# Moving the normalised activations to other byte offsets, with a shifted copy for the low-part products

## Chip, cores and metric

One Trainium2 chip, one NeuronCore. The metric is the device time of one execution in microseconds; less is better. The kernel before takes 793.53 us (median of 3 runs, 793.42 to 794.03). The granted TensorE clock of the profiled execution is 1.000 throughout, the 2.4 GHz level.

## What is computed

Two transformer blocks on 256 tokens of width 1024, everything in float32:

```python
# first_block: 16 meta tokens in front
h = h + concat([pool, forgetting_attention, stick_breaking_attention]) @ w_out
h = h + (silu(a @ w_gate) * (a @ w_up)) @ w_down      # a = rmsnorm(h)
# second_block
x = x + 0.5 * rmsnorm(swiglu(rmsnorm(x), w_ffn1_in, w_ffn1_out))
x = x + rmsnorm(mixer(rmsnorm(x)))                    # convolution and mLSTM
x = x + 0.5 * rmsnorm(swiglu(rmsnorm(x), w_ffn2_in, w_ffn2_out))
```

So there are three FFNs with hidden width 2816, an attention block and a mixer. Activations and weights enter each product split into two parts of float32r, hi and lo, and three of the four partial products are summed: hi by hi, hi by lo, lo by hi.

## The kernel before

**Weights.** All large weights come as a stream of 129 units of 128 x 2048 float32 (1 MB), which SyncE loads into three slots `raw`. For every unit ScalarE writes `whi` (a rounding copy, L695) and VectorE writes `wlo = raw - whi` (L1023), three slots each. `hi_ready`, `lo_ready` and `unit_used` count units made and used.

**An FFN** (`ffn(f)`, f = 0, 1, 2) has 11 groups of 256 hidden columns; a group is a gate unit, an up unit and a down unit of weights. TensorE (`ffn` in the tensor block) takes them in an order written out by hand: the first gate unit (`first_paired_unit`), up(0), then group(1) written out flat, then groups 2 to 10 as a hardware loop (`pe.Fori`), each group being gate(g), up(g), down(g - 1), and a last down unit. In gate and up

- `hi_products` are 16 matmuls with 512 moving columns: the moving operand is `xn[norm][:, kt, :, :]`, the hi and lo block of one k-tile next to each other, the stationary operand a 128 x 128 slice of `whi`;
- `lo_products` are 16 matmuls with 256 moving columns: the moving operand is the hi block `xn_hi[norm][:, kt, :]`, the stationary operand a slice of `wlo`.

In down (`rows_tile`) the roles are the other way round: 24 matmuls whose moving operand is 512 columns of `whi` or `wlo` and whose stationary operand is a slice of `hhi` or `hlo`.

**The mixer** has 12 weight units. Ten of them go through `columns_tile` or `first_columns_unit` (48 matmuls each, 256 moving columns of `xn_hi[2]` or `xn_lo[2]`, stationary slices of `whi` or `wlo`); the two units of kind "v" go through `tokens_tile` (48 matmuls each, moving 256 columns of the weights, stationary slices of `xn_hi[2]` and `xn_lo[2]`).

**Where things lie.** `raw`, `whi`, `wlo` (three each, 8192 bytes a partition), `xa` (17408) and `ya` (16384), `hhi` and `hlo` (2048 each) are allocated one after the other, and every size is a multiple of 512 bytes. So all of them start at the same residue of the byte address modulo 512. A weight slice starts a multiple of 512 bytes into its buffer: it is at "the weights' residue", called residue 0 here. Other operands are given by how many bytes past it they start, modulo 512. The normalised activations of norm k lie in `xa`, from element `XN_AT[k][0]` on, and k-tiles follow each other every 2048 bytes, hi block first, lo block 1024 bytes behind it. `XN_AT` is 80 elements for all four norms, which is residue 320. The `hhi`, `hlo` and `ya` slices that serve as stationary operands of down and out are at residue 0.

**ScalarE at the head of an FFN** (`ffn` in the scalar block): the whi copy of unit0 + 2 (`split_ahead(unit0)`), `gate_lo` (L875) that takes the first gate product out of PSUM, in the second and third FFN two `root_of_x` (L705 to L735), a table load (L896), the whi copy of unit0 + 3, `up_lo` (L883), the whi copy of unit0 + 4, the silu of group 0 (L879). VectorE's wlo of unit0 + 3 waits for that whi copy, and behind it on VectorE stands `up(0)` (L1278), for which TensorE's up(1) waits (`up_out`).

```python
XN_AT = ((80, SEQ),) * 4
        for at, far in XN_AT:
            line = xa_line[:, at:at + KT * 2 * SEQ if far == SEQ else at + 2 * far]
```

Of the kernel before, what the change touches and what calls it, by code (L numbers as in the profile page):

```python
# [31 lines left out]
F32 = mybir.dt.float32  # L32
F32R = mybir.dt.float32r
ALU = mybir.AluOpType
ACT = mybir.ActivationFunctionType
# [4 lines left out]
KT = D // P  # L40
META = 16
SEQ = 256
# [3 lines left out]
GROUPS = FF // 256  # L46
UNIT = 2048
SLOTS = 3
XN_AT = ((80, SEQ),) * 4
XN_HI = (0, 0, 0, 0)  # L50
EPS = 1e-6
NEG = -1e30
# [218 lines left out]
def build_blocks(nc, x_in, meta_in, wstream, ident_in, vecs_in, small_in, const_in, rows_in, out):  # L271
    with ExitStack() as ctx:  # L272
# [3 lines left out]
        def sem(name):  # L276
            return ctx.enter_context(nc.semaphore(name))


        ps = ctx.enter_context(nc.psum_tensor("ps", [P, 8, 512], F32))  # L280
        raw = [sb(f"raw{s}", [P, UNIT]) for s in range(SLOTS)]
        whi = [sb(f"whi{s}", [P, UNIT], F32R) for s in range(SLOTS)]
        wlo = [sb(f"wlo{s}", [P, UNIT], F32R) for s in range(SLOTS)]
        xa = sb("xa", [P, KT, 2 * TOK], F32R)
        ya = sb("ya", [P, KT, 2 * SEQ], F32R)
# [144 lines left out]
        xn_hi = [xn[k][:, :, n, :] for k, n in enumerate(XN_HI)]  # L430
        xn_lo = [xn[k][:, :, 1 - n, :] for k, n in enumerate(XN_HI)]

        xa_hi, xa_lo = xa[:, :, 0:TOK], xa[:, :, TOK:2 * TOK]
        ps_line = ps[:].rearrange("p b c -> p (b c)")

# [10 lines left out]
        unit_used = sem("unit_used")  # L446
# [30 lines left out]
        xa_hi_ready = sem("xa_hi_ready")  # L477
# [78 lines left out]
        up_lo_out = sem("up_lo_product_out")  # L556
        up_out = sem("up_out_of_psum")
        silu_done = sem("silu_done")
        h_done = sem("h_done")
        hhi_done = sem("h_hi_done")  # L560
        hlo_done = sem("h_lo_done")
# [120 lines left out]
        def _(act):  # L682
# [14 lines left out]
            def split_ahead(n):  # L697

                if n + 2 < UNITS:
                    split(n + 2, (n + 2) % SLOTS, (n + 2) // SLOTS)  # L700
# [167 lines left out]
            def ffn(f):  # L868
                base, unit0 = f * GROUPS, U_FFN[f]

                def gate_lo(g, unit):
                    act.wait_ge(unit_used, unit + 1)
                    if not isinstance(g, int) or base + g:
                        act.wait_ge(h_done, g + base)
                    nc.scalar.activation(silu, products(4)[1], ACT.Copy).then_inc(gate_lo_out, 1)  # L875

                def gate(g):
                    act.wait_ge(gate_scaled, g + (base + 1))
                    nc.scalar.activation(silu, silu, ACT.Silu).then_inc(silu_done, 1)  # L879

                def up_lo(unit):
                    act.wait_ge(unit_used, unit + 1)
                    nc.scalar.activation(up_sum, products(6)[1], ACT.Copy).then_inc(up_lo_out, 1)  # L883

                def hidden_hi(g, down_before, last=False):
                    act.wait_ge(h_done, g + (base + 1))
                    if down_before is not None and not last:
                        act.wait_ge(unit_used, down_before + 1)
                    nc.scalar.activation(ya[:, 0:2, 0:SEQ] if last else hhi[:], hact, ACT.Copy).then_inc(hhi_done, 1)  # L889

                split_ahead(unit0)
                gate_lo(0, unit0)
                if f:
                    for tt in range(TT):
                        root_of_x((0, 1, 3)[f], tt)
                nc.scalar.preload_act_table_set("silu_and_others")  # L896
                split_ahead(unit0 + 1)
                up_lo(unit0 + 1)
                split_ahead(unit0 + 2)
                gate(0)  # L900
                hidden_hi(0, None)

                def group(g, last=False):

                    for j in range(3):

                        n = g * 3 + (unit0 - 1 + j)
                        c = unit0 + 1 + j
                        if last and j == 2:
                            hidden_hi(g, n, True)  # L910
                        if isinstance(g, int):
                            if n != unit0 + 2:
                                split_ahead(n)
                        else:
                            split(n + 2, c % SLOTS, g + c // SLOTS)
                        if j == 0:
                            gate_lo(g, n)
                        if j == 1:
                            gate(g)
                            up_lo(n)  # L920
                        if j == 2 and not last:
                            hidden_hi(g, n)

                group(1)
                with act.Fori(2, GROUPS - 1) as g:
                    group(g)
                group(GROUPS - 1, True)
                nc.scalar.preload_act_table_set("natural_log_exp_and_others")  # L928
                split_ahead(unit0 + N_FFN - 1)
# [15 lines left out]
            for kind, i in SECOND:  # L945
                if kind in ("munit", "mout"):
                    split_ahead((U_MIX if kind == "munit" else U_MIXOUT) + i)
                if kind == "munit":
                    what = MIX_KIND[i]
                    if what == "v":  # L950
                        act.wait_ge(root_ready, R_BEFORE[2] + 2 * TT)
                        act.wait_ge(unit_used, U_MIX + i + 1)
                        for tt in range(TT):
                            ins = nc.scalar.activation(mv[:, tt, (i - 2) * SEQ:(i - 1) * SEQ], two(UNIT_BANK[i])[:, tt, :], ACT.Copy,
                                                       scale=stat[:, S_RSTD[2] + tt:S_RSTD[2] + tt + 1])
# [32 lines left out]
                if kind == "ml_weigh":  # L988
                    act.wait_ge(decay_row, 1)
                    act.wait_ge(ml_scored, i + 1)  # L990
                    for tt in range(TT):
                        for dr in range(2):
                            _, d, n = DIRECTION[tt, dr]
                            ins = nc.scalar.activation(dm[:, tt, d:d + n], ps[:, 4 + tt, d:d + n], ACT.Exp,
                                                       bias=max_neg[:, tt, dr, i:i + 1])
# [480 lines left out]
        def _(pe):  # L1476
            def mm(o, lhsT, rhs, start, stop):
                return nc.tensor.matmul(o, lhsT, rhs, start=start, stop=stop, skip_group_check=True)  # L1478
# [310 lines left out]
            def ffn(f):  # L1789
                base, unit0 = f * GROUPS, U_FFN[f]  # L1790

                norm = (0, 1, 3)[f]

                def hi_products(bank, slot, start, spread=False):

                    for kt in range(KT):
                        if spread and kt == KT // 2:
                            spread_rstd(norm, 2)
                        for a in range(2):
                            w = slice(kt * 256 + a * P, kt * 256 + (a + 1) * P)  # L1800
                            ins = mm(two(bank + a), whi[slot][:, w], xn[norm][:, kt, :, :], start and kt == 0, not start and kt == KT - 1)
                    return ins

                def lo_products(bank, slot, start):

                    for kt in range(KT):
                        for a in range(2):
                            w = slice(kt * 256 + a * P, kt * 256 + (a + 1) * P)
                            ins = mm(ps[:, bank + a, 0:SEQ], wlo[slot][:, w], xn_hi[norm][:, kt, :], start and kt == 0, not start and kt == KT - 1)
                    return ins  # L1810

                def gate(g, unit, slot, first):
                    pe.wait_ge(gate_out, g + base)
                    pe.wait_ge(hi_ready, unit)
                    hi_products(4, slot, True, first)
                    pe.wait_ge(lo_ready, unit + 1)
                    lo_products(4, slot, False).then_inc(unit_used, 1)

                def up(g, unit, slot):
                    if not isinstance(g, int) or g:  # L1820
                        pe.wait_ge(up_out, g + base)
                    pe.wait_ge(lo_ready, unit + 1)
                    lo_products(6, slot, True)
                    hi_products(6, slot, False).then_inc(unit_used, 1)

                def down(g, unit, slot, first, last):

                    pe.wait_ge(lo_ready, unit + 1)
                    pe.wait_ge(hlo_done, g + (base + 1))
                    for a in range(2):  # L1830
                        ins = rows_tile(slot, a, hhi[:, a, :], hlo[:, a, :], first and a == 0, last and a == 1)
                    ins.then_inc(unit_used, 1)

                pe.wait_ge(lo_ready, unit0 + 1)
                first_paired_unit(4, unit0 % SLOTS, norm).then_inc(unit_used, 1)
                up(0, unit0 + 1, (unit0 + 1) % SLOTS)

                def group(g, first):
                    n = g * 3 + (unit0 - 1)
                    gate(g, n, (unit0 + 2) % SLOTS, first)  # L1840
                    up(g, n + 1, unit0 % SLOTS)
                    down(g - 1, n + 2, (unit0 + 1) % SLOTS, first, False)

                group(1, True)
                with pe.Fori(2, GROUPS) as g:
                    group(g, False)
                n = unit0 + N_FFN - 1
                pe.wait_ge(lo_ready, n + 1)
                pe.wait_ge(hlo_done, base + GROUPS)
                rows_last_unit(n % SLOTS, [(ya[:, a, 0:SEQ], ya[:, a, SEQ:2 * SEQ]) for a in range(2)], (1, 2, 4)[f])  # L1850
# [175 lines left out]
```

## Time and profile before

| what | value |
|---|---|
| median of 3 runs | 793.53 us |
| profiled execution, its own time | 793.85 us |
| its span, first to last instruction | 792.0 us |
| TensorE busy | 781.6 us |
| VectorE / ScalarE busy | 533.2 us / 429.3 us |
| DMA | 141.16 MB, 178 GB/s over the span |

A matmul in the trace has a start and a modelled end, and the matmuls overlap, so what a product costs TensorE is read from starts: the time from one start to a later one, divided by the number of products between (called the pace here). A row of the timeline merges equal neighbours; its first number is the start of the first, its last the count.

### The profile page before, as it was taken

What the parts mean: (1) busy time and instruction counts of PE and PEld (TensorE: products, weight loads), DVE (VectorE), ACT (ScalarE), POOL (GpSimd) and SP (SyncE); (2) the same over time, 40 slices, a digit from 0 to 9 for tenths busy, and PEclk for the clock granted to TensorE, in tenths of its full rate; (3) what the DMA queues carried; (4) which work ended last, traced back from release to release, by engine and by line L of the source; (5) the groups of instructions that cost most, each with busy time, mean ns of one, the idle gap of its engine ahead of it and who ended that gap; (6) DMA issues with size and microseconds to landing.
All of it is one profiled execution on the core that took longest, in us unless ns stands there. A gap on an engine that the chain in (4) does not pass through costs nothing.

```text
span 792.0 us, 12209 instructions
## 1 busy us (share of the span) xinstructions
PE 781.6 (99%) x4710; PEld 687.9 (87%) x4710; DVE 533.2 (67%) x628; ACT 429.3 (54%) x565; POOL 28.3 (4%) x35
## 2 busy tenths in 40 slices
PE   9999999999999999999999999999999999999997
PEld 8989988888888888888888887999988888888885
DVE  7866657766666667866666566766977766666665
ACT  6556657544544448744544447565557654454444
POOL 0000000000000000000000000002520000000000
PEclk9999999999999999999999999999999999999999
DMA  9633433645555553665545554452444664555521
GB/s 335 235 110 112 143 115 128 245 166 205 191 183 209 175 196 110 238 224 199 198 176 209 183 188 159 142 204 108 161 165 162 221 223 166 205 192 183 208 106 54
DMA packets 20797, 141.16 MB, mean 178 GB/s; under 512 B 2448, under 2 KB 2704, under 8 KB 4384
## 3 DMA queue, kind: packets, MB, share of 16 engines
q1 hardware_dynamic: 20192, 138.65, 48.8%
q0 software_dynamic: 576, 2.10, 0.8%
q8 instruction: 21, 0.34, 0.2%
q14 instruction: 8, 0.07, 0.0%
HBM read 139.69 MB, written 1.05 MB: 178 GB/s over the span
## 4 chain that ended last, share of the span: by engine, by line
PE 94%; ACT 2%; DVE 2%; issue 1%; DMA 1%; SPq 0%; DVEq 0%; ACTq 0%
PE ps L1478 93%; ACT whi L695 1%; PE ps L1484 1%; DMA raw<-wstream 1%; DVE x L1227 0%; ACT squared L710 0%; DVE xa L1034 0%; PE ps L1707 0%; DVE wlo L1023 0%; PE ps L1677 0%; PE ps L1926 0%; DVE xg L1222 0%; DVEq L272 0%; ACT L928 0%; PE ps L1709 0%
## 5 line engine op out<-in xcount | busy, mean ns | idle before, releaser
L1478 PE MATMUL ps<-xa,whi 128*128 128x512 f32 (+2 forms) x1744 | 377.4, 347 | 0.0
L1023 DVE TENSOR_TENSOR wlo<-raw,whi 128x2048 fp32r<-128x2048 f32 x128 | 293.6, 2295 | 82.2 <-ACT whi L695 82.2
L1478 PEld LDWEIGHTS ps<-xa,whi 128*128 128x128 f32 x1744 | 299.6, 188 | 41.4 <-issue 2.1
L695 ACT ACTIVATE whi<-raw 128x2048 fp32r<-128x2048 f32 x128 | 244.2, 1909 | 6.9 <-PE ps L1478 6.8
L1478 PE MATMUL ps<-xa,wlo 128*128 128x256 f32 (+1 forms) x1376 | 219.8, 278 | 0.0
L1478 PEld LDWEIGHTS ps<-xa,wlo 128*128 128x128 f32 x1376 | 187.9, 188 | 2.8
L1478 PE MATMUL ps<-wlo,hhi 128*128 128x512 f32 x240 | 93.5, 390 | 0.0
L1478 PE MATMUL ps<-whi,hlo 128*128 128x512 f32 x240 | 93.5, 390 | 0.0
L1478 PE MATMUL ps<-whi,hhi 128*128 128x512 f32 x240 | 93.5, 390 | 0.0
L889 ACT ACTIVATE hhi<-arena 128x512 fp32r<-128x512 f32 x30 | 19.0, 633 | 88.4 <-PE ps L1478 81.9
L875 ACT ACTIVATE arena<-ps 128x512 f32<-128x512 f32 x33 | 19.7, 597 | 85.5 <-PE ps L1478 85.4
L883 ACT ACTIVATE arena<-ps 128x512 f32<-128x512 f32 x33 | 19.7, 597 | 71.4 <-PE ps L1478 71.4
L1478 PE MATMUL ps<-whi,ya 128*128 128x512 f32 x176 | 56.5, 395 | 0.0
L1478 PEld LDWEIGHTS ps<-whi,hhi 128*128 128x128 f32 x240 | 45.1, 188 | 9.6
L1478 PEld LDWEIGHTS ps<-wlo,hhi 128*128 128x128 f32 x240 | 45.1, 188 | 9.5
L1478 PEld LDWEIGHTS ps<-whi,hlo 128*128 128x128 f32 x240 | 45.1, 188 | 9.5
L1269 DVE TENSOR_TENSOR arena<-ps,arena 128x512 f32<-128x512 f32 x33 | 22.8, 691 | 39.6 <-ACT arena L875 39.6
L1278 DVE TENSOR_TENSOR arena<-ps,arena 128x512 f32<-128x512 f32 x33 | 22.8, 691 | 36.6 <-ACT arena L883 36.6
L1290 DVE TENSOR_TENSOR hlo<-arena,hhi 128x512 fp32r<-128x512 f32 x30 | 20.8, 692 | 37.8 <-ACT hhi L889 37.7
L1478 PEld LDWEIGHTS ps<-whi,ya 128*128 128x128 f32 x176 | 33.1, 188 | 6.8
L1478 PE MATMUL ps<-wlo,ya 128*128 128x512 f32 x88 | 34.5, 393 | 0.0
L1478 PE MATMUL ps<-arena 64*128 64x144 f32 (+11 forms) x190 | 24.3, 340 | 1.8 <-DVE arena L1067 1.3
(221 smaller groups left out, 531.6 us busy)
## 6 DMA issues: line engine op xcount, KB each, us to landing
raw<-wstream SPq DMA_DIRECT2D x128, 1024.0 KB, 4.8
gain_row<-rows_in POOLq DMA_DIRECT2D x4, 512.0 KB, 3.9
x<-x_in SPq DMA_DIRECT2D x2, 512.0 KB, 4.0
raw<-wstream SPq DMA_DIRECT2D x2, 512.0 KB, 5.8
out<-x SPq DMA_DIRECT2D x4, 256.0 KB, 2.1
xg<-const_in SPq DMA_DIRECT2D x1, 912.0 KB, 11.8
small<-small_in SPq DMA_DIRECT2D x1, 152.0 KB, 6.1
arena<-meta_in SPq DMA_DIRECT2D x1, 64.0 KB, 4.5
```

Of the source, the lines that this page charges most:

```text
L695: nc.scalar.activation(whi[slot][:], raw[slot][:], ACT.Copy).then_inc(hi_ready, 1)
L875: nc.scalar.activation(silu, products(4)[1], ACT.Copy).then_inc(gate_lo_out, 1)
L883: nc.scalar.activation(up_sum, products(6)[1], ACT.Copy).then_inc(up_lo_out, 1)
L889: nc.scalar.activation(ya[:, 0:2, 0:SEQ] if last else hhi[:], hact, ACT.Copy).then_inc(hhi_done, 1)
L1023: nc.vector.tensor_tensor(wlo[slot][:], raw[slot][:], whi[slot][:].bitcast(F32), ALU.subtract).then_inc(lo_ready, 1)
L1269: nc.vector.tensor_tensor(silu, products(4)[0], silu, ALU.add).then_inc(gate_out, 1)
L1278: nc.vector.tensor_tensor(up_sum, products(6)[0], up_sum, ALU.add).then_inc(up_out, 1)
L1290: nc.vector.tensor_tensor(lo, hact, hi.bitcast(F32), ALU.subtract).then_inc(hlo_done, 1)
L1478: return nc.tensor.matmul(o, lhsT, rhs, start=start, stop=stop, skip_group_check=True)
L1484: ins = nc.tensor.transpose(turn_place(k, kt)[:, tt * P:(tt + 1) * P], x[:, tt, kt * P:(kt + 1) * P], ident[:])
```

## The change

The normalised activations of the three FFNs (norms 0, 1 and 3) move to residue 0, those of the mixer (norm 2) to residue 192. At the head of each FFN ScalarE copies the eight hi blocks into `ya`, 16 elements in, so that the copy lies at residue 64; it is one ACTIVATE of 128 x 2048, and it waits for the hi blocks and for the last unit before the FFN to be used. From group 1 on the lo products take their moving operand from this copy; the first unit and up(0) take it from `xn_hi` as before. TensorE waits for the copy once in each FFN, ahead of the lo products of group 1.

```diff
-XN_AT = ((80, SEQ),) * 4
+XN_AT = ((0, SEQ), (0, SEQ), (48, SEQ), (0, SEQ))
+FAR = 16
...
+        x_far = ya[:, :, FAR:FAR + SEQ]
...
                 split_ahead(unit0)
+                act.wait_ge(xa_hi_ready, KT * ((0, 1, 3)[f] + 2))
+                act.wait_ge(unit_used, unit0)
+                nc.scalar.activation(x_far, xn_hi[(0, 1, 3)[f]].bitcast(F32), ACT.Copy).then_inc(far_ready, 1)
                 gate_lo(0, unit0)
...
-                def lo_products(bank, slot, start):
+                def lo_products(bank, slot, start, of):
...
-                            ins = mm(ps[:, bank + a, 0:SEQ], wlo[slot][:, w], xn_hi[norm][:, kt, :], start and kt == 0, not start and kt == KT - 1)
+                            ins = mm(ps[:, bank + a, 0:SEQ], wlo[slot][:, w], of[:, kt, :], start and kt == 0, not start and kt == KT - 1)
...
                     pe.wait_ge(lo_ready, unit + 1)
-                    lo_products(4, slot, False).then_inc(unit_used, 1)
+                    if first:
+                        pe.wait_ge(far_ready, f + 1)
+                    lo_products(4, slot, False, x_far).then_inc(unit_used, 1)
...
-                    lo_products(6, slot, True)
+                    lo_products(6, slot, True, xn_hi[norm] if isinstance(g, int) and g == 0 else x_far)
```

No instruction moves against another on any engine apart from the three added ones. ScalarE at the head of the second FFN, before (whi copy of unit0 + 2, gate_lo, the two roots, table load, whi copy of unit0 + 3, up_lo):

```order
179 L695 ACTIVATE whi<-raw 128x2048 [waits unit_used,unit_landed1]
180 L875 ACTIVATE arena<-ps 128x512 [waits h_done,unit_used]
181 L705 ACTIVATE squared,stat<-x 128x1024 [waits x_written]
182 L733 ACTIVATE stat<-stat,eps 128x1 [waits act_step]
183 L735 ACTIVATE stat<-stat 128x1 [waits act_step]
184 L705 ACTIVATE squared,stat<-x 128x1024 [waits x_written]
185 L733 ACTIVATE stat<-stat,eps 128x1 [waits act_step]
186 L735 ACTIVATE stat<-stat 128x1 [waits act_step]
187 L896 ACT_TABLE_LOAD
188 L695 ACTIVATE whi<-raw 128x2048 [waits unit_used,unit_landed2]
189 L883 ACTIVATE arena<-ps 128x512 [waits unit_used]
```

and in the change (line numbers behind the edits are 3 to 8 higher):

```order
180 L698 ACTIVATE whi<-raw 128x2048 [waits unit_used,unit_landed1]
181 L897 ACTIVATE ya<-xa 128x8x256 [waits unit_used,xa_hi_ready]
182 L878 ACTIVATE arena<-ps 128x512 [waits h_done,unit_used]
183 L708 ACTIVATE squared,stat<-x 128x1024 [waits x_written]
184 L736 ACTIVATE stat<-stat,eps 128x1 [waits act_step]
185 L738 ACTIVATE stat<-stat 128x1 [waits act_step]
186 L708 ACTIVATE squared,stat<-x 128x1024 [waits x_written]
187 L736 ACTIVATE stat<-stat,eps 128x1 [waits act_step]
188 L738 ACTIVATE stat<-stat 128x1 [waits act_step]
189 L902 ACT_TABLE_LOAD
190 L698 ACTIVATE whi<-raw 128x2048 [waits unit_used,unit_landed2]
191 L886 ACTIVATE arena<-ps 128x512 [waits unit_used]
```

The copy stands between the first whi copy and gate_lo, and all that follows stands behind it. TensorE in the same FFN, from up(0) to the first products of down(0), before:

```order
762 L1478 MATMUL ps<-xa,wlo 128x256 x15
763 L1478 MATMUL ps<-xa,whi 128x512 x16
764 L1478 MATMUL ps<-xa,whi 128x512 [waits unit_hi_ready,gate_out_of_psum]
765 L1478 MATMUL ps<-xa,whi 128x512 x7
766 L1478 MATMUL ps<-diag,exact 128x128 [waits diag_ready] x2
767 L1478 MATMUL ps<-xa,whi 128x512 x8
768 L1478 MATMUL ps<-xa,wlo 128x256 [waits unit_lo_ready]
769 L1478 MATMUL ps<-xa,wlo 128x256 x15
770 L1478 MATMUL ps<-xa,wlo 128x256 [waits unit_lo_ready,up_out_of_psum]
771 L1478 MATMUL ps<-xa,wlo 128x256 x15
```

and in the change:

```order
767 L1484 MATMUL ps<-xa,whi 128x512 x8
768 L1484 MATMUL ps<-ya,wlo 128x256 [waits far_copy_of_hi_activations_ready,unit_lo_ready]
769 L1484 MATMUL ps<-ya,wlo 128x256 x15
770 L1484 MATMUL ps<-ya,wlo 128x256 [waits unit_lo_ready,up_out_of_psum]
771 L1484 MATMUL ps<-ya,wlo 128x256 x15
```

The same products in the same order: the moving operand of the lo products is `ya` now, and the first of them has one more semaphore to wait for.

## Rows read from the trace of the kernel before

**Rows 1.** The page: busy time of each engine, and the chain that ended last

```profile
PE 781.6 (99%) x4710; PEld 687.9 (87%) x4710; DVE 533.2 (67%) x628; ACT 429.3 (54%) x565; POOL 28.3 (4%) x35
...
PE 94%; ACT 2%; DVE 2%; issue 1%; DMA 1%; SPq 0%; DVEq 0%; ACTq 0%
```

**Rows 2.** Timeline of TensorE, one loop iteration: start, us, line, names, form, count

```profile
154.77 3.84 PE L1478 MATMUL ps<-xa,whi 128*128 128x512 f32 x16
158.45 3.79 PE L1478 MATMUL ps<-xa,wlo 128*128 128x256 f32 x32
162.08 3.82 PE L1478 MATMUL ps<-xa,whi 128*128 128x512 f32 x16
165.74 0.39 PE L1478 MATMUL ps<-whi,hhi 128*128 128x512 f32 x1
...
171.19 3.84 PE L1478 MATMUL ps<-xa,whi 128*128 128x512 f32 x16
```

**Rows 3.** Groups of TensorE by form: names, count, busy us, mean ns

```profile
L1478 PE MATMUL ps<-xa,whi 128*128 128x512 f32 x1008 | 241.7, 392 | 0.0
L1478 PE MATMUL ps<-xa,wlo 128*128 128x256 f32 x1264 | 189.3, 277 | 0.0
```

**Rows 4.** Timeline of TensorE, up(0) and group 1 of the second FFN (flat code)

```profile
317.42 5.67 PE L1478 MATMUL ps<-xa,whi 128*128 128x512 f32 x24
...
325.21 3.93 PE L1478 MATMUL ps<-xa,wlo 128*128 128x256 f32 x32
328.98 0.39 PE L1478 MATMUL ps<-xa,whi 128*128 128x512 f32 x1
```

**Rows 5.** Timeline of TensorE, first and last-but-one row of a mixer columns unit

```profile
536.55 0.40 PE L1478 MATMUL ps<-xa,whi 128*128 128x256 f32 x2
...
542.08 0.28 PE L1478 MATMUL ps<-xa,wlo 128*128 128x256 f32 x1
```

**Rows 6.** Timeline of TensorE, second and last row of both v units

```profile
510.72 0.28 PE L1478 MATMUL ps<-wlo,xa 128*128 128x256 f32 x1
...
516.14 0.28 PE L1478 MATMUL ps<-whi,xa 128*128 128x256 f32 x1
...
517.04 0.28 PE L1478 MATMUL ps<-wlo,xa 128*128 128x256 f32 x1
...
522.25 0.28 PE L1478 MATMUL ps<-whi,xa 128*128 128x256 f32 x1
```

**Rows 7.** Timeline of TensorE: an attention q tile, then the first unit of FFN 1

```profile
57.67 0.28 PE L1478 MATMUL ps<-xa,wlo 128*128 128x256 f32 x1
...
60.15 0.28 PE L1478 MATMUL ps<-xa,wlo 128*128 128x256 f32 x1
...
127.58 0.28 PE L1478 MATMUL ps<-xa,wlo 128*128 128x256 f32 x1
...
130.19 1.98 PE L1478 MATMUL ps<-xa,whi 128*128 128x256 f32 x16
```

**Rows 8.** Timeline of ScalarE, then of VectorE, head of the second FFN; idle in brackets

```profile
313.72 1.90 ACT L695 ACTIVATE whi<-raw 128x2048 fp32r<-128x2048 f32 x1
...
316.73 1.06 ACT L705 ACTIVATE squared<-x 128x1024 f32<-128x1024 f32 x1 [0.40 <-DVE x L1247]
...
321.37 1.91 ACT L695 ACTIVATE whi<-raw 128x2048 fp32r<-128x2048 f32 x1
323.19 0.58 ACT L883 ACTIVATE arena<-ps 128x512 f32<-128x512 f32 x1
...
323.38 2.29 DVE L1023 TENSOR_TENSOR wlo<-raw,whi 128x2048 fp32r<-128x2048 f32 x1 [1.82 <-ACT whi L695]
325.59 0.68 DVE L1278 TENSOR_TENSOR arena<-ps,arena 128x512 f32<-128x512 f32 x1
```

**Rows 9.** Timeline of ScalarE, heads of the first and of the third FFN

```profile
137.93 0.60 ACT L883 ACTIVATE arena<-ps 128x512 f32<-128x512 f32 x1 [1.89 <-PE ps L1478]
...
610.73 0.60 ACT L875 ACTIVATE arena<-ps 128x512 f32<-128x512 f32 x1 [1.72 <-PE ps L1478]
```

More of the change, by code:

```diff
@@ L558, in build_blocks @@
         silu_done = sem("silu_done")
+        far_ready = sem("far_copy_of_hi_activations_ready")
         h_done = sem("h_done")
```

## Prediction

> **What bounds the kernel.** I read the page's busy shares first and then its chain of waits [rows 1]: TensorE is busy for 781.6 of 792.0 us and makes up 94% of the chain that ended last. Nothing waits longer than TensorE works, so a change counts by what it does to the pace of TensorE's products, or by a wait that it puts in front of them. The modelled lengths (392 ns, 277 ns) overlap and say nothing of a pace [rows 3], so the next view is the timeline, by starts.
>
> One loop iteration of an FFN [rows 2]: the gate's 16 hi products take 158.45 - 154.77 = 3.68 us, 230.0 ns each; the 32 lo products of gate and up 3.63 us, 113.4 ns each; the up's 16 hi products 3.66 us, 228.8 ns each; the 24 products of down 5.45 us, 227.1 ns each. Hi products and down products have the same 512 moving columns. The first have their moving operand at residue 320 against the slice that is loaded for the next product, the second at residue 0. Twice a lo product is 226.8 ns, so down runs at what seems to be the floor, and the hi products about 2.3 ns above it.
>
> With 256 moving columns the picture is less simple. At residue 320 they run at 113.4 ns in the loop [rows 2], and the same products with the same slots in the flat group 1 at 3.77 us / 32 = 117.8 ns [rows 4]. Flat code can be fast too: the first unit of FFN 1 (residue 320, flat) takes 2.61 us / 23 = 113.5 ns a product [rows 7]. The mixer's columns unit (residue 320) takes 5.53 us / 47 = 117.7 ns [rows 5]; all of the columns units but the first look like it. The v units have moving weights against stationary activations, residue 192: the first takes 5.42 us / 46 = 117.8 ns, the second 5.21 us / 46 = 113.3 ns [rows 6]. So there are two steady paces, a short one (113.3) and a long one (117.8), a whole unit stays in one of them, and something besides the residue picks which. That is the weak spot of this forecast.
>
> **The change part by part.**
>
> *FFN hi products from residue 320 to 0.* There are 1008 [rows 3]. Their mean is (230.0 + 228.8) / 2 = 229.4 ns, down's is 227.1 [rows 2]. I take down's value, because it has the same shape, the same weight buffers and the residue to which they go: 1008 x 2.3 ns = -2.3 us. Ends: 0, if the residue isn't the reason, and 1008 x 2.7 = -2.7 us, if they reach 226.7. The copy at residue 64 plays no part in it. All of it is on the path.
>
> *Loop lo products from 320 to 64.* 27 iterations x 32 = 864 products. 320 and 64 differ by 256 bytes. The trace has no run of 256-column products at 64 alone; in the attention tiles, where the residue runs through 0, 64, 128 and on, nothing sets 64 apart from 320 [rows 7]. I take no change, 0; ends: 0 and, if they fall to the long pace, 864 x 4.4 = +3.8 us. The 96 lo products of the flat group 1 stay at 117.8 [rows 4]; end: the short pace, -0.4 us.
>
> *First unit and up(0) from 320 to 0.* 64 products with 256 columns in each FFN, flat, now at residue 0, which is only bounded by the attention q tile, whose products go through residues 0, 64, 128 and on: 2.48 us / 21 = 118.1 ns [rows 7]. The tile is the nearest row; I take it, with 0.5 ns for what it mixes in: 118.6. Of the 192 products some 40 (FFN 1's first unit behind its waits) are at 113.5 now, the other 152 at 117.8: 40 x 5.1 + 152 x 0.8 = +0.3 us. Ends: all short, -0.7 us; all at 120 (the long pace and half as much again), +0.6 us.
>
> *Mixer from 320 to 192.* Ten columns units with 480 products. The first is at the short pace behind a wait, nine (432 products) at the long one [rows 5]. The only rows at residue 192 are the two v units, one long, one short [rows 6]; so I take half: 216 x 4.4 ns = -1.0 us. Ends: 0 and -1.9 us. The two v units themselves go from 192 to 320, which is what the columns units have now: the short one becomes long, 48 x 4.5 = +0.2 us; ends 0 and +0.2.
>
> *The copy.* Three ACTIVATEs of 128 x 2048. The whi copy has that shape: 1.91 us long, the next instruction starts 323.19 - 321.37 = 1.82 us behind it [rows 8]. What is behind it on ScalarE moves by up to 1.82 us. In the first FFN ScalarE has 1.89 us of idle time ahead of up_lo, in the third 1.72 us ahead of gate_lo [rows 9]: hidden, and with that cover gone the next instructions come about 0.1 us late, which no one waits for. In the second FFN the copy starts at 313.72 + 1.82 = 315.54, gate_lo at 317.36 and the first square of x 0.49 us later (gate_lo's pitch), 317.85 instead of 316.73; the 0.40 us of idle there [rows 8] is used up, and 1.1 us of delay is left. It carries over to the whi copy of unit0 + 3 (322.5), the wlo behind it on VectorE (324.5 to 326.8) and up(0), L1278, which ends at 325.59 + 0.68 + 1.1 = 327.4 instead of 326.3. TensorE's up(1) wants it 16 lo products into the run that starts at 325.21 [rows 4], at 325.21 + 16 x 0.1178 = 327.1. So TensorE waits about 0.35 us once: +0.35. Ends: 0 and +0.8 (delay of 1.5 us, if nothing of the idle time helps). The products behind it are late by the same wait, so I count no second one. The copy itself is ready some 8 us ahead of the wait for it, and raw slots, DMAs and the GpSimd queue see nothing.
>
> Sum: -2.3 + 0 + 0.3 - 1.0 + 0.2 + 0.35 = -2.45 us. From the profiled execution's own 793.85 us that is 791.4; it stands 0.3 us above the median of the runs, so for the median **791.1 us**. A measurement of this kernel can tell about 0.2%, 1.6 us, from no change.
>
> **Rivals.**
>
> *The long pace takes the loop.* In the loop the lo products run at the short pace at 320, in flat code mostly at the long one [rows 2, 4]; what picks it isn't seen. If they go into the long pace behind hi products at residue 0, or 64 isn't like 320, each of 864 costs 4.4 ns: +3.8 us. If the mixer finds no better pace either (+1.0), 791.1 + 3.8 + 1.0 = 795.9 us, slower than before. It decides from about 560 of the 864 products on, where 2.45 us are eaten. For it: the same products show both paces. Against it: all 27 iterations look like the one shown, and 64 is 320 less 256. Chance 0.12.
>
> *The mixer gains nothing, the rest holds.* Columns at 192 stay at 117.8 like the first v unit [rows 6], and the first units are at the costly end: 791.1 + 1.0 + 0.3 = 792.4 us. Chance 0.16.
>
> *Addresses don't matter.* Then the 2.3 ns of the hi products come from their place in the program (the first ones behind the loop's branch, the slots), and the change leaves only its copy: 793.53 + 0.35 = 793.9 us. Against it: the up's hi products don't stand behind a branch and are at 228.8 all the same [rows 2]. Chance 0.10. The Trainium skill says so in effect: "TensorE: Matmul & The Clock Gate", "Step-by-step: what each phase is for", has two independent SBUF read ports, and loading the next tile's weights takes no read bandwidth from the running matmul; "SBUF — State Buffer", "Who interferes with whom", has it that TensorE never waits on anyone. By that rule no residue would change a pace. The trace doesn't show that the ports are the cause of the two paces, but it shows the same product at 113.4 and at 117.8 ns [rows 2, 4], which the rule leaves unexplained.
>
> *All of the mixer and the flat group go short:* 791.1 - 1.0 - 0.5 = 789.6 us. Chance 0.07.
>
> **How the numbers follow.** The forecast has 0.55. Its own range is 790.0 to 792.3. The range for 8 in 10 goes down to 789.4, which takes in most of the good case, and up to 794.4, which takes in the mixer rival and the no-effect rival; the long-pace rival is left out. Faster by over 0.2% (under 791.9 us): forecast and good case, 0.55 + 0.07, less what of the forecast's own range lies above, plus a little of the mixer rival: 0.60. Within 0.2%: the mixer rival, the no-effect rival and the edges, 0.28. Slower: 0.12.
>
> **What would show it.** Hi products of the loop at 226.7 to 227.1 ns in gate and up, iterations shorter by about 32 x 2.3 = 0.07 us (16.42 us from gate to gate before, 16.35 after). Lo products in the loop still 113.4 ns; at 117.8 the long-pace rival is right. Mixer columns units of 48 products at 5.44 us (short) or 5.65 us (long), the v units at the long pace. In the second FFN one TensorE wait of some 0.35 us for L1278's successor in the middle of group 1's lo products, none in the other two. The forecast is wrong if hi products stay at 229, or if TensorE waits for ScalarE or VectorE anywhere by over 1 us.

## The result, and the profile after

The change takes 795.82 us (median of 12 runs, 795.5 to 796.34) against 793.83 us of the kernel before on the same chip (12 runs, 793.42 to 794.37): a ratio of 1.0025, 95% interval 1.0018 to 1.0033. It is slower by 0.25%. The profiled execution took 796.34 us, with a span of 794.4 us.

The page of the change, busy time of each engine and the chain that ended last:

```profile
PE 783.3 (99%) x4710; PEld 691.1 (87%) x4710; DVE 533.0 (67%) x628; ACT 434.9 (55%) x568; POOL 28.3 (4%) x35
...
PE 88%; DVE 4%; ACT 3%; issue 2%; POOL 1%; DMA 1%; SPq 0%; DVEq 0%; ACTq 0%; POOLq 0%
```

Beside [rows 1] TensorE has the same 4710 products and 1.7 us more work, ScalarE 5.6 us more (its three copies). The chain now takes detours over VectorE, ScalarE and GpSimd, but TensorE is still busy nearly all the time, so the pace decides again. The same loop iteration as in [rows 2], by the timeline of TensorE (start, us, line, names, form, count):

```profile
155.10 3.79 PE L1484 MATMUL ps<-xa,whi 128*128 128x512 f32 x16
158.72 3.93 PE L1484 MATMUL ps<-ya,wlo 128*128 128x256 f32 x32
162.50 3.82 PE L1484 MATMUL ps<-xa,whi 128*128 128x512 f32 x16
166.15 0.39 PE L1484 MATMUL ps<-whi,hhi 128*128 128x512 f32 x1
...
171.59 0.61 PE L1484 MATMUL ps<-xa,whi 128*128 128x512 f32 x2
```

| part of the iteration | before, from [rows 2] | after | difference |
|---|---|---|---|
| gate hi, 16 | 3.68 us | 3.62 us, 226.3 ns each | -0.06 |
| lo, 32 | 3.63 us, 113.4 ns each | 3.78 us, 118.1 ns each | +0.15 |
| up hi, 16 | 3.66 us | 3.65 us, 228.1 ns each | -0.01 |
| down, 24 | 5.45 us | 5.44 us | -0.01 |
| gate to gate | 16.42 us | 16.49 us | +0.07 |

Times 27 iterations the row differences are about +1.9 us, which is all of the loss. Taken over every start in the 27 iterations the lo products went from 113.3 to 117.9 ns (864 of them: +3.9 us), the hi products from 229.4 to 227.55 ns on the mean (864: -1.6 us) and down's from 227.2 to 226.7 ns (648: -0.3 us): +2.0 us. A row's start is rounded to 0.01 us, so a pace read from one row's length is good to about 0.6 ns for 16 products and 0.3 ns for 32; where tenths of a nanosecond matter, means over all 27 iterations are given.

The second FFN, TensorE from the hi products ahead of group 1's lo products on (the counterpart of [rows 4]):

```profile
324.35 2.09 PE L1484 MATMUL ps<-xa,whi 128*128 128x512 f32 x8
326.28 4.18 PE L1484 MATMUL ps<-ya,wlo 128*128 128x256 f32 x32
330.30 2.00 PE L1484 MATMUL ps<-xa,whi 128*128 128x512 f32 x8
```

ScalarE there, in the change (the counterpart of [rows 8]):

```profile
316.51 1.91 ACT L897 ACTIVATE ya<-xa 128x2048 fp32r<-128x2048 f32 x1
...
323.42 1.92 ACT L698 ACTIVATE whi<-raw 128x2048 fp32r<-128x2048 f32 x1
```

and VectorE:

```profile
325.43 2.29 DVE L1029 TENSOR_TENSOR wlo<-raw,whi 128x2048 fp32r<-128x2048 f32 x1 [2.47 <-ACT whi L698]
327.64 0.68 DVE L1284 TENSOR_TENSOR arena<-ps,arena 128x512 f32<-128x512 f32 x1
```

The copy is the row at 316.51. Behind it the whi copy of unit0 + 3 comes at 323.42 instead of 321.37, 2.05 us later, while TensorE's lo products come 1.07 us later (326.28 instead of 325.21): ScalarE lost 1.0 us against TensorE. VectorE's L1284 ends at 328.32, and TensorE wanted it at 326.28 + 16 x 0.1178 = 328.16. The 32 lo products take 4.02 us instead of 3.77; the two long pitches inside (329 and 222 ns from start to start) add 0.3 us. The rest of the run shows something else: the 15 pitches ahead of the wait are 118.0 ns on the mean, the 15 behind it 113.3. The last 14 products, up to the hi products at 330.30, TensorE:

```profile
328.72 1.75 PE L1484 MATMUL ps<-ya,wlo 128*128 128x256 f32 x14
```

So the pace can turn at a short wait in the middle of a run.

### The profile page after: what moved, and what is told of

Read it like the earlier page. It is cut to its first block, busy times and chain, and to the rows that moved or that the text cites. A ratio compares the mean times of both kernels' runs of the same rounds, so it can differ in the third digit from the quotient of the medians.

```text
span 794.4 us, 12218 instructions
## 1 busy us (share of the span) xinstructions
PE 783.3 (99%) x4710; PEld 691.1 (87%) x4710; DVE 533.0 (67%) x628; ACT 434.9 (55%) x568; POOL 28.3 (4%) x35
## 4 chain that ended last, share of the span: by engine, by line
PE 88%; DVE 4%; ACT 3%; issue 2%; POOL 1%; DMA 1%; SPq 0%; DVEq 0%; ACTq 0%; POOLq 0%
PE ps L1484 86%; DVE wlo L1029 1%; ACT whi L698 1%; DMA raw<-wstream 1%; PE ps L1490 1%; POOL arena L674 0%; POOL arena L677 0%; DVE x L1233 0%; ACT squared L713 0%; DVE xa L1040 0%; ACT xa L744 0%; DVE arena L1450 0%; PE ps L1713 0%; ACT squared L708 0%; PE ps L1683 0%
## 5 line engine op out<-in xcount | busy, mean ns | idle before, releaser
L1484 PEld LDWEIGHTS ps<-ya,wlo 128*128 128x128 f32 x960 | 117.3, 188 | 2.6 <-DVE arena L1284 0.3
L1484 PE MATMUL ps<-ya,wlo 128*128 128x256 f32 x960 | 118.2, 280 | 0.1
L1484 PE MATMUL ps<-xa,wlo 128*128 128x256 f32 (+1 forms) x416 | 105.7, 282 | 0.0
L1484 PEld LDWEIGHTS ps<-xa,wlo 128*128 128x128 f32 x416 | 74.7, 189 | 0.1
L1284 DVE TENSOR_TENSOR arena<-ps,arena 128x512 f32<-128x512 f32 x33 | 22.8, 691 | 37.9 <-ACT arena L886 37.9
```

The lines of the kernel that those rows point to most:

```text
L1284: nc.vector.tensor_tensor(up_sum, products(6)[0], up_sum, ALU.add).then_inc(up_out, 1)
```

## The runs that look for the cause

Two theories for the lo products. **The entry theory**: the pace of a run of 256-column products is set by the products ahead of it; behind hi products at residue 320 it is short, behind hi products at residue 0 long, and 64 is as good as 320. **The address theory**: 64 isn't like 320, the copy itself lies badly.

### The change with every activation at 320 again

Only the copy at residue 64 is left of the change.

```diff
-XN_AT = ((0, SEQ), (0, SEQ), (48, SEQ), (0, SEQ))
+XN_AT = ((80, SEQ), (80, SEQ), (80, SEQ), (80, SEQ))
```

> The change with all activations back at residue 320, so only the copy at residue 64 and its use by the lo products are left. Entry theory (which pace a run of 256-column products takes is settled by the products ahead of it, and hi products at 320 lead into the short one): loop lo products at 113.3 ns as in the kernel before, hi products 229.4, time 793.8 plus about 0.3 for the wait in the second FFN, 794.1 us. Residue theory (64 is a residue of the long pace, unlike 320): loop lo products at 117.8 ns, 864 x 4.5 ns = +3.9, about 798 us.

Measured: 793.99 us, 1.0002 of before (0.9993 to 1.0011). Its loop iteration, timeline of TensorE:

```profile
154.68 3.84 PE L1484 MATMUL ps<-xa,whi 128*128 128x512 f32 x16
158.37 3.79 PE L1484 MATMUL ps<-ya,wlo 128*128 128x256 f32 x32
161.99 3.82 PE L1484 MATMUL ps<-xa,whi 128*128 128x512 f32 x16
```

3.62 / 32 = 113.1 ns a lo product with the moving operand at 64. Over all 27 iterations it is 113.3 ns, the same as before. The address theory falls. Of the copy only its one wait is left: the second FFN's group 1 takes 0.4 us longer, and nothing else of it shows. Here the pace doesn't turn at that wait; the last 14 lo products behind it stay at 1.65 us / 14 = 117.9 ns:

```profile
327.64 1.81 PE L1484 MATMUL ps<-ya,wlo 128*128 128x256 f32 x14
329.29 0.39 PE L1484 MATMUL ps<-xa,whi 128*128 128x512 f32 x1
```

### The change with the copy at 320, and at 192

```diff
-FAR = 16
+FAR = 80
```

> The change with the copy 320 bytes past the weights' residue instead of 64 (FAR = 80); hi products stay at residue 0. Entry theory: hi products at residue 0 lead into the long pace whichever of 64 and 320 follows, loop lo products at 117.8 ns, time as the change, 795.8 us. Residue theory: 320 is the residue that had 113.3 ns in the loop before, so 113.3 again, 795.8 - 3.9 = 791.9 us, and a little less because the up's first hi products lose their 230 to 236 ns.

Measured: 796.0 us, 1.0027 (1.0015 to 1.0038). Timeline of TensorE, the loop iteration:

```profile
155.00 3.79 PE L1484 MATMUL ps<-xa,whi 128*128 128x512 f32 x16
158.62 3.93 PE L1484 MATMUL ps<-ya,wlo 128*128 128x256 f32 x32
162.39 3.82 PE L1484 MATMUL ps<-xa,whi 128*128 128x512 f32 x16
```

The lo products are at 320, where the kernel before has 113.4 ns, and take 3.77 / 32 = 117.8 ns. With the run above this is the crossing that was wanted: in the loop the residue of the lo products (64 or 320) changes nothing, and that of the hi products ahead decides, 113.3 ns behind 320 and 117.9 behind 0 (means over the 27 iterations, which agree within 0.1 ns).

With `FAR = 48` (192):

> The change with the copy at residue 192 (FAR = 48). In the changed kernel's mixer seven of nine full columns units at residue 192 ran at 113.3 ns and both v units at 320 at 117.8. If 192 is a better residue for 256-column products than 64 and 320, loop lo products at 113.3 ns, up's hi products at 226.7 from the first on: 795.8 - 3.9 - 0.7 = 791.2 us. If the entry by hi products at residue 0 alone decides, 117.8 ns and 795.8 us.

Measured: 796.18 us, 1.0033 (1.0021 to 1.0045). The lo products take 117.8 ns over the loops as well, and the up's hi products behind them 229.5 ns on the mean, 1 ns more than with 64.

### The mixer alone at 192

```diff
-XN_AT = ((80, SEQ),) * 4
+XN_AT = ((80, SEQ), (80, SEQ), (48, SEQ), (80, SEQ))
```

> The kernel before with the mixer's activations alone at residue 192; FFNs at 320, no copy. By the two traces TensorE's products in the mixer get 1.1 us shorter and new waits for VectorE behind GpSimd's tap chain take 1.0 us back: 793.8 - 0.1, no change that can be measured. Rival: the waits come from the later start of the mixer in the changed kernel and not from the faster products; then 793.8 - 1.1 = 792.7 us.

Measured: 793.66 us, 0.9998 (0.9989 to 1.0007). The mixer's stretch is 0.15 us shorter, here and in the change alike. In the change six of the nine long-paced columns units run at the short pace (the expectation for 192 above counted seven); an early and the last lo product of one unit, 45 products apart, TensorE:

```profile
538.53 0.28 PE L1484 MATMUL ps<-xa,wlo 128*128 128x256 f32 x1
...
543.63 0.28 PE L1484 MATMUL ps<-xa,wlo 128*128 128x256 f32 x1
```

5.10 us / 45 = 113.3 ns, against 117.7 in [rows 5]. But TensorE then runs into VectorE. Further on in the change, TensorE:

```profile
565.92 0.28 PE L1484 MATMUL ps<-exact,ident_r 128*128 128x256 f32 x1
566.39 0.47 PE L1484 MATMUL ps<-xa,whi 128*128 128x256 f32 x2 [0.19 <-DVE arena L1401]
...
578.65 0.60 PE L1934 MATMUL ps<-ident,arena 128*128 128x128 f32 x4
579.40 0.50 PE L1484 MATMUL ps<-whi,ya 128*128 128x512 f32 x1 [0.15 <-DVE arena L1395]
```

VectorE just ahead of the first of these waits:

```profile
563.30 2.28 DVE L1029 TENSOR_TENSOR wlo<-raw,whi 128x2048 fp32r<-128x2048 f32 x1
565.50 0.74 DVE L1401 TENSOR_TENSOR arena<-ps,arena 128x256 f32<-128x256 f32 x2
```

and the waits of TensorE from 500 to 590 us of the change (line waited for: us in total, times, longest); before has the diagonal's alone:

```profile
PE ps L1484 <- DVE diag L1264: 0.3, 1, 0.3
PE ps L1484 <- DVE arena L1401: 0.2, 1, 0.2
PE ps L1484 <- DVE arena L1395: 0.2, 1, 0.2
```

The view counts only idle time between modelled ends; by starts the waits are longer. From 565.92 to 566.39 are 0.47 us where the kernel before has 0.12, and from 578.65 the four transposes hold 0.4 us more than before. The run with the mixer alone at 192 has both waits too, at the same places in the program. The sum over the starts of the change's mixer: columns products -1.19 us, v units +0.20, these two waits +0.82, rest 0. VectorE's work there was a few tenths of a microsecond ahead of TensorE, so no more than that could be gained. The run with the copy at 320 bears it out: its columns products take 1.9 us less than before, its waits grow, and its mixer is 0.4 us shorter.

That run shows a second thing. Its mixer is the change's, instruction for instruction and at the same residues, but all nine of those units run at the short pace, and the first unit, short in the change, at the long one. Residues and the order of the products alone don't settle the pace of a unit there.

### The last hi product in front of the lo products split

In the change, the last hi product of gate becomes two of 256 columns, still at residue 0; this asks whether another way into the lo products changes their pace.

```diff
+                            if start and kt == KT - 1 and a == 1:
+                                for half in range(2):
+                                    ins = mm(two(bank + a)[:, half, :], whi[slot][:, w], xn[norm][:, kt, half, :], False, False)
+                                continue
```

> The change with one product of each gate split: the last hi product (512 columns, residue 0) is done as two of 256 columns with the same weights, so that the lo products behind it are entered another way at no arithmetic cost (2 x 113.3 = 226.7 ns if both go at the short pace). Entry theory: the way in decides, so a different way in can move the 32 lo products of an iteration to 113.3 ns; if it does, 864 x 4.5 ns less, 795.8 - 3.9 - 0.7 = 791.2 us. If this entry too leads into the long pace, 117.8 ns stays and the time is 795.8 us plus 27 x 0.01. A theory in which moving and loaded residue alone decide has 795.8 us for certain.

Measured: 796.11 us, 1.0026 (1.0016 to 1.0037), lo products at 117.9 ns. It doesn't; this way in leads to the long pace too.

### One residue for a whole FFN: 0, 192, 448, 128

These are the kernel before with one line changed, no copy, the mixer left at 320:

```diff
-XN_AT = ((80, SEQ),) * 4
+XN_AT = ((0, SEQ), (0, SEQ), (80, SEQ), (0, SEQ))
```

and 48, 112 or 32 in place of the 0.

> The kernel before with the FFN activations at residue 0 and no copy: hi and lo products both at 0 (mixer at 320). Hi products at 226.7 ns, at least in the gate. Entry theory: the lo products at the long pace or worse (the changed kernel's up(0) ran at 120.0 ns at residue 0): 864 x 4.5 to 6.7 ns more, less 1.8 for the hi products, 795.9 to 797.8 us. If the copy in ya is what harms, lo products at 113.3 and 791.9 us.

> The kernel before with the FFN activations at residue 192 and no copy. The mixer's columns units at 192 run mostly at 113.3 ns. If 192 is the best residue all round, hi products at 226.7 and lo products at 113.3: 793.8 - 2.3 - 0.5 = 791.0 us. If only residue 0 gives hi products their floor, hi products stay near 229, lo products at 113.3: 793.3 to 793.8 us.

> The kernel before with the FFN activations at residue 448 and no copy. In the attention tiles of both traces the lo products at 448 had the shortest pace of all residues (122.7 ns for 272 columns, floor 120.4). Same two cases as at 192: 791.0 us if hi products reach 226.7 and lo products keep 113.3, 793.3 to 793.8 if hi products stay near 229. If modulo 256 is what counts, the same result as 192.

> The kernel before with the FFN activations at residue 128 and no copy. Modulo 128 it is like 0; modulo 256 it isn't like any residue run so far (0: hi 226.7, lo 120; 64 and 320: hi 229, lo 113.3; 192 and 448: hi 233, lo 113.7). If the trade between the two widths is general, hi at 226.7 and lo at 117.8 to 120, 797.5 us as at residue 0; a residue good for both would give 113.3 and 226.7, 791.5 us.

Measured: 797.49 us at 0 (1.0045, 1.0031 to 1.0059), 797.52 at 192 (1.0047, 1.0034 to 1.0061), 797.53 at 448 (1.0045, 1.0031 to 1.0059), 802.6 at 128 (1.0111, 1.0095 to 1.0126). The loop iteration of the first, by the timeline of TensorE:

```profile
154.53 3.79 PE L1478 MATMUL ps<-xa,whi 128*128 128x512 f32 x16
158.15 4.00 PE L1478 MATMUL ps<-xa,wlo 128*128 128x256 f32 x32
161.99 3.82 PE L1478 MATMUL ps<-xa,whi 128*128 128x512 f32 x16
```

of the second:

```profile
154.58 3.89 PE L1478 MATMUL ps<-xa,whi 128*128 128x512 f32 x16
158.31 3.80 PE L1478 MATMUL ps<-xa,wlo 128*128 128x256 f32 x32
161.95 3.89 PE L1478 MATMUL ps<-xa,whi 128*128 128x512 f32 x16
```

and of the one at 128:

```profile
155.36 3.89 PE L1478 MATMUL ps<-xa,whi 128*128 128x512 f32 x16
159.08 3.96 PE L1478 MATMUL ps<-xa,wlo 128*128 128x256 f32 x32
162.88 3.90 PE L1478 MATMUL ps<-xa,whi 128*128 128x512 f32 x16
```

At 0: gate hi 3.62 / 16 = 226.3 ns, lo 3.84 / 32 = 120.0. At 192: hi 3.73 / 16 = 233.1, lo 3.64 / 32 = 113.8, and 448 the same within 0.1 ns. At 128: hi 3.72 / 16 = 232.5, lo 3.80 / 32 = 118.8. So the hi products do follow the residue, modulo 256 as far as 192 and 448 show. At 192 and 448 the lo products have the short pace behind hi products that are 4 ns slower, so a slow hi pace isn't what takes the short pace away. The case on record for residue 0 came (795.9 to 797.8 us); for 192, 448 and 128 neither of the two cases did, since all of them put the hi products at 226.7 or near 229 ns.

At 192 throughout, the flat group 1 shows that the products ahead don't settle the pace either. Its lo products in the first and in the second FFN, with the same products ahead of them at the same residue, TensorE:

```profile
141.75 3.80 PE L1478 MATMUL ps<-xa,wlo 128*128 128x256 f32 x32
145.39 0.85 PE L1478 MATMUL ps<-xa,whi 128*128 128x512 f32 x3
...
326.40 3.93 PE L1478 MATMUL ps<-xa,wlo 128*128 128x256 f32 x32
330.17 1.09 PE L1478 MATMUL ps<-xa,whi 128*128 128x512 f32 x4
```

3.64 / 32 = 113.8 ns in the first (and in the third), 3.77 / 32 = 117.8 in the second. At 448 it is the first FFN that has the long pace. So the entry theory holds for the loop, where all 27 iterations agree; in flat code something further back counts too.

### The last k-tiles at 320, the others at 0

If the products right ahead of a run set its pace, a few hi products at 320 just ahead of the lo products should bring the short pace back. In the change, the last k-tile of the FFN activations is put at 320 (two hi products a gate or up unit), and the lo products of that k-tile are read there, so that the copy has seven tiles. (The lines that place the tile are left out here.)

```diff
-                            ins = mm(ps[:, bank + a, 0:SEQ], wlo[slot][:, w], of[:, kt, :], start and kt == 0, not start and kt == KT - 1)
+                            ins = mm(ps[:, bank + a, 0:SEQ], wlo[slot][:, w], (xn_hi[norm] if kt >= KT - 1 else of)[:, kt, :], start and kt == 0, not start and kt == KT - 1)
```

> The change with the last k-tile of the FFN activations at residue 320 instead of 0 (it needs no copy, so the copy has seven tiles). The lo products of the gate are now entered behind two hi products at 320; the other 14 of 16 hi products stay at 0. Entry theory: loop lo products at 113.3 ns, hi products at 0 at 226.7 and the up's first ones without their 230 to 236 ns: against the kernel before 28 x 2.4 x 27 = -1.8 us and -0.3 in down, +0.5 in the first units, +0.3 wait, -0.1 mixer, 792.4 us. If two products don't suffice or the pace is set by something else, 117.8 ns and 795.8 us.

Measured: 797.02 us, 1.0044 (1.0031 to 1.0058). Two products at 320 don't bring it back: lo products at 117.9 ns, and the two hi products themselves took 237 and 235 ns. With the changes of residue inside the unit the hi products take 229.0 ns on the mean instead of the change's 227.6, 1.2 us over the loops, which is why it is slower than the 795.8 us on record for this case.

The same with the copy on VectorE behind the diagonals instead of on ScalarE:

```diff
-                act.wait_ge(xa_hi_ready, KT * ((0, 1, 3)[f] + 2))
-                act.wait_ge(unit_used, unit0)
-                nc.scalar.activation(x_far, xn_hi[(0, 1, 3)[f]].bitcast(F32), ACT.Copy).then_inc(far_ready, 1)
...
                 rstd_diagonals((0, 1, 3)[f])
+                dve.wait_ge(xa_hi_ready, KT * ((0, 1, 3)[f] + 2))
+                dve.wait_ge(unit_used, unit0)
+                nc.vector.tensor_copy(x_far[:, 0:KT - 1, :], x_first[:, 0:KT - 1, :].bitcast(F32)).then_inc(far_ready, 1)
```

> As e9_late1, with the copy on VectorE behind its diagonals, where it is idle for 1.8 us in the second FFN, instead of on ScalarE. The wait theory (the added 0.3 us in the second FFN is ScalarE's delay of the whi copy behind the copy) expects no TensorE wait of over 0.1 us there and 0.3 us less than e9_late1. If VectorE's copy takes longer than its idle time the wait stays: equal to e9_late1.

Measured: 797.44 us, 1.0047 (1.0033 to 1.006); the intervals of the two overlap, and the 0.3 us less that were expected didn't come. They weren't there to gain: the run before had only one long pitch left (216 ns, 0.1 us) and took 3.80 us for these 32 products, because its copy is shorter and the pace turned short at that wait. Now the wait in group 1 of the second FFN is gone; its lo products, TensorE:

```profile
326.45 1.81 PE L1496 MATMUL ps<-ya,wlo 128*128 128x256 f32 x14
...
330.22 1.09 PE L1496 MATMUL ps<-xa,whi 128*128 128x512 f32 x4
```

330.22 - 326.45 = 3.77 us, what the kernel before has in [rows 4]. So the delay came from the copy's place on ScalarE.

With the last two k-tiles at 320 (four hi products a unit), copy on VectorE:

> As e10_late1_dve, with the last two k-tiles at residue 320, so four hi products stand ahead of the lo products. If two products are too few to turn the pace but four are enough, lo products at 113.3 ns here and 117.8 there. If two suffice already, 2 x 2.3 ns x 2 x 27 = +0.25 us against e10_late1_dve. If neither does, about 795.5 us.

Measured: 794.47 us, 1.0009 (1.0000 to 1.0018). Timeline of TensorE, the loop iteration:

```profile
154.96 3.82 PE L1496 MATMUL ps<-xa,whi 128*128 128x512 f32 x16
158.62 1.52 PE L1496 MATMUL ps<-ya,wlo 128*128 128x256 f32 x12
159.98 0.62 PE L1496 MATMUL ps<-xa,wlo 128*128 128x256 f32 x4
...
162.24 3.84 PE L1496 MATMUL ps<-xa,whi 128*128 128x512 f32 x16
...
171.39 0.84 PE L1496 MATMUL ps<-xa,whi 128*128 128x512 f32 x3
```

The lo products take 3.62 / 32 = 113.1 ns: four products at 320 ahead do what two don't, and at once, from the first lo product on (159.98 - 158.62 = 1.36 us for 12). That is the entry theory for the loop shown from its other side. It leaves open whether four products at 320 are enough by themselves: in the loop of the kernel before, too, the gate's hi products at 320 follow products at residue 0 (those of down), and its first four take 236, 235, 232 and 232 ns. The four here show the same 237, 235, 232 and 232; with one k-tile only the first two of these appear; and in the flat group 1 of the kernel before, whose lo products are long, the eight hi products at 320 stand behind the diagonal's products and, further back, others at 320, and are 316, 226, 233, 236, 229, 232, 225 and 230 ns apart, without that passage. "A whole passage from 0 to 320 ahead" fits the long group 1 as well, "products at 320 ahead" doesn't; but no run was made to tell the two apart, and this run's own group 1, which has four at 320 behind others at 0, is long at 3.77 us all the same (its four take 231, 226, 233 and 236 ns).

The change of residue inside the unit costs what the floor gives: the four products at 320 took 232 to 237 ns each, the first five of up at 0 228 to 236, and gate to gate are 16.43 us, before 16.42.

None of the twelve beats the kernel before; the mixer alone at 192 and the copy with every activation at 320 equal it, and the last comes within 0.1%.

## Why the prediction was wrong

The forecast was 791.1 us with a range of 789.4 to 794.4; measured were 795.82. Point by point:

**Hi products, -2.3 us.** The mechanism was right: it is the residue, they reach the floor of down (gate 226.7 ns over the loops, down itself 226.7 then). The size was off: -1.6 us in the loops where 864 x 2.3 = -2.0 were counted. The first six of up's hi products came behind long-paced lo products and took 228 to 236 ns, 0.8 us in all; that the others reached 226.7 and not the 227.1 of the sum gave 0.4 us back.

**Loop lo products, "I take no change, 0".** This is the step that failed. Its high end, +3.8 us, is what came: +3.9. The step weighed only the move of the lo products themselves, 320 to 64, and on that it was right (113.3 ns at 64). But the change also moved the products ahead of them, and in the loop that sets the pace: the same lo products at 320 fell to 117.9 ns behind hi products at 0. The trace of before showed the warning, two paces for one product [rows 2, 4], and the text called it the weak spot. The rival with this very condition stood in the forecast at 0.12 and outside the range; with nothing in the rows against it but that 27 iterations looked alike, all of them behind hi products at 320, it deserved more.

**First unit and up(0), +0.3 us.** Start against start, from the first unit to the hi products of up(0), the three FFNs take 0.11, 0.12 and 0.02 us longer, +0.25 us: the size was right, in part by luck. At residue 0 these 256-column products take 120 ns, the end called the long pace and half as much again, about +0.5 us by themselves; the rest of it went into waits that were there before and got shorter (FFN 1: two pitches of 184 and 222 ns, 0.17 us less in all). The first unit of FFN 1, the counterpart of [rows 7], TensorE of the change:

```profile
127.88 0.28 PE L1484 MATMUL ps<-xa,wlo 128*128 128x256 f32 x1
...
130.51 0.28 PE L1484 MATMUL ps<-xa,wlo 128*128 128x256 f32 x1
130.63 2.08 PE L1484 MATMUL ps<-xa,whi 128*128 128x256 f32 x16
132.55 2.08 PE L1484 MATMUL ps<-xa,wlo 128*128 128x256 f32 x16
134.47 5.63 PE L1484 MATMUL ps<-xa,whi 128*128 128x512 f32 x24
```

(130.63 - 127.88) / 23 = 119.6 ns where 113.5 were, and 1.92 us / 16 = 120.0 ns for the next two runs. The mixed tile that I took as the nearest row, 118.6, hid that.

**Mixer, -1.0 + 0.2 us.** The sizes were right, -1.19 and +0.20, with six of nine units short where half was assumed; the end missed, since 0.82 us went into two waits for VectorE. The step had no look at how far ahead VectorE was. Net -0.15 us, and the run with the mixer alone agrees.

**The copy, +0.35 us.** Right in place and mechanism: one wait in the second FFN for `up(0)`, 0.25 to 0.3 us, none in the others. With the copy on VectorE it went away.

**The rivals.** *The long pace takes the loop* came true, and its 795.9 us is the measured time within 0.1. Of its two conditions the first holds (hi products at residue 0 ahead), the second (64 isn't like 320) doesn't. It assumed that the mixer finds no better pace; the mixer did, and lost it to waits, which gives nearly the same sum. The closeness is partly luck: the rival is +2.35 us on 793.53, measured are +1.99 on 793.83. *Addresses don't matter* falls: by the residue alone the gate's hi products go from 226.3 ns (0) to 233.1 (192). So the measurement decides against what the Trainium skill has in "TensorE: Matmul & The Clock Gate", "Step-by-step: what each phase is for", of two independent read ports, as far as one would draw from it that no address changes a pace; what happens inside the port, no run shows. *All short* didn't come, *the mixer gains nothing* came in its result only.

**What stays open.** Why a run behind hi products at 320 is short in the loop but long in the flat group 1 (3.77 us / 32 before, the same in the run with the last two k-tiles at 320), why the same products at the same residues take either pace in flat code (group 1 at 192, the mixer), why a wait turns the pace in one run and not in another, and what in the engine keeps a pace once it is taken. The cause of the loss is shown as the residue of the hi products ahead in the loop; how it acts isn't. A version with only gate's last k-tiles at 320 and up all at 0 wasn't tried; by the pitches above it could bring about 1 us at best, and it needs a second place for those tiles.

## What to carry to other kernels

Where one product shows two paces in one trace, don't price a change of address by that product's own address alone: look at what runs ahead of it, count whether the change moves that too, and give both paces a real chance. A better pace for one kind of product can cost more on the next kind: here 2 ns on 864 products were bought with 4.5 ns on 864 others. And before a faster TensorE is counted as gain, look how far ahead of it the engine is that feeds its next wait.

## What the runs showed of the hardware

With stationary slices of float32r at residue 0 and the granted clock at the 2.4 GHz level, moving operand 512 columns (hi) or 256 columns (lo), means over the 27 loop iterations:

| residue of both | hi, ns (gate / up) | lo, ns |
|---|---|---|
| 0 | 226.7 / 228.4 | 119.8 |
| 128 | 232.8 / 233.5 | 118.8 |
| 192 and 448 | 233.3 / 233.0 | 113.7 |
| 320 (the kernel before) | 230.1 / 228.7 | 113.3 |

| hi at | lo at | lo, ns |
|---|---|---|
| 320 | 64 | 113.3 |
| 0 | 64 | 117.9 |
| 0 | 320 | 117.9 |
| 0 | 192 | 117.8 |
| 0, the last four at 320 | 64, the last two k-tiles at 320 | 113.3 |
| 0, the last two at 320 | 64, the last k-tile at 320 | 117.9 |

No run has 512-column products at residue 64.

Unexpected were three things. The fastest residue for 512 columns is the slowest for 256. In the loop the pace of a run of 32 products follows the residue of the products ahead of it, more than two of them, and stays to the end of the run; but it isn't tied to residues alone, since in the second FFN of the change the pace turned from 118.0 to 113.3 ns at a wait in the middle of a run, and flat code shows both paces for the same products at the same residues. And 512-column products pay for what stood ahead of them: behind products at another residue or lo products at the long pace the first four to six take 228 to 241 ns (one of them 224) where the steady ones at residue 0 take 226.7. That is not a cost of every switch: twelve lo products at 64 followed by four at 320 all take 113.3 ns, and with everything at residue 0, without any switch, the first five of up's hi products take 228 to 236 ns behind the slow lo products.
